# Rotary embedding of q and k: the swapped halves by DMA between SBUF partitions instead of a permutation matmul

## What is computed

```
def rope(x):                      # x[..., 64]
    x1, x2 = x[..., :32], x[..., 32:]
    return concatenate([x1 * cos - x2 * sin, x2 * cos + x1 * sin], axis=-1)

qa = rope(rms(aq, a_q_norm)); ka = rope(rms(ak, a_k_norm))   # 4 heads x 2 each
qc = rope(cq);                kc = rope(ck) * 64 ** -0.5     # 4 heads each
w  = softmax(qa0 ka0) - lam * softmax(qa1 ka1); y_a = rms(w @ va)
```

## Time and profile before

| | |
|---|---|
| median of the runs | 3362.06 us |
| the profiled execution, its own time | 3362.12 us |
| its span | 3360.3 us |
| PE busy | 3253.8 us, 97%, 14858 instructions |
| PE weight load busy | 2604.9 us, 78% |
| DVE busy | 1762.4 us, 52% |
| ACT busy | 1281.6 us, 38% |
| POOL busy | 28.7 us, 1% |
| mean granted TensorE clock | 0.986 |
| share of PE in the chain that ended last | 83% |
| HBM weight stream (q1) | 283.15 MB, 29.5% of 16 DMA engines |

### The profile page before, as it was taken

One profiled execution on the slowest core, in us unless ns is written; L12 is line 12 of the kernel. 1 busy time (PEld: TensorE's weight loads), 2 busy tenths in 40 slices (PEclk: granted clock), 3 DMA queues, 4 the chain that ended last, 5 costly groups with the idle time before them and its releaser, 6 DMA issues.

```text
span 3360.3 us, 37192 instructions
## 1 busy us (share of the span) xinstructions
PE 3253.8 (97%) x14858; PEld 2604.9 (78%) x14858; DVE 1762.4 (52%) x2893; ACT 1281.6 (38%) x1952; POOL 28.7 (1%) x57
## 2 busy tenths in 40 slices
PE   7999999999999999999999999999999986999998
PEld 6888877677788888888877677878888764878886
DVE  6333688645463336433487755364334665873333
ACT  4222446533342224322356544243233365343222
POOL 0000000000000000000000000000000000000000
PEclk9999999999999999999999999999999997999999
DMA  4333321222233332333222232323333542223332
GB/s 134 100 99 90 100 82 58 78 82 86 90 94 101 94 94 88 107 95 100 88 89 68 67 90 80 94 83 106 100 95 89 99 63 42 67 85 103 94 97 72
DMA packets 282077, 297.75 MB, mean 89 GB/s; under 512 B 9776, under 2 KB 270256, under 8 KB 281904
## 3 DMA queue, kind: packets, MB, share of 16 engines
q1 hardware_dynamic: 277408, 283.15, 29.5%
q0 software_dynamic: 3536, 10.55, 1.0%
q10 hardware_dynamic: 960, 1.67, 0.1%
HBM read 293.24 MB, written 2.10 MB: 88 GB/s over the span
## 4 chain that ended last, share of the span: by engine, by line
PE 83%; DVE 10%; ACT 5%; issue 1%; DMA 1%; DVEq 0%; SPq 0%; ACTq 0%
PE bank L218 83%; DVE k_sc L180 2%; ACT k_sc L214 2%; DVE k_wl L170 1%; DVE k_sc L170 1%; PE bank L224 1%; ACT k_wh L214 1%; ACT L208 1%; DVE k_sc L184 1%; DMA k_raw<-in_ffn_w_gate 0%; DVE k_sc L196 0%; DVE k_sm L175 0%; DVE k_x L180 0%; ACT k_sc L213 0%; DVE k_sc L175 0%
## 5 line engine op out<-in xcount | busy, mean ns | idle before, releaser
L170 DVE TENSOR_TENSOR k_wl<-k_raw,k_wh 128x1024 fp32r<-128x1024 f32 x545 | 654.5, 1204 | 1142.8 <-ACT k_wh L214 1140.1
L218 PE MATMUL bank<-k_xh,k_wh 128*128 128x512 f32 x2376 | 956.9, 403 | 3.8 <-ACT k_xh L214 1.6
L214 ACT ACTIVATE k_wh<-k_raw 128x1024 fp32r<-128x1024 f32 x545 | 563.6, 1039 | 973.3 <-PE bank L218 704.6
L218 PE MATMUL bank<-k_xl,k_wh 128*128 128x512 f32 x2376 | 927.6, 390 | 1.7 <-DVE k_xl L170 1.7
L218 PE MATMUL bank<-k_xh,k_wl 128*128 128x512 f32 x2376 | 927.6, 390 | 1.2 <-DVE k_wl L170 1.2
L218 PEld LDWEIGHTS bank<-k_xh,k_wh 128*128 128x128 f32 x2376 | 447.5, 188 | 116.1 <-issue 18.8
L218 PEld LDWEIGHTS bank<-k_xl,k_wh 128*128 128x128 f32 x2376 | 447.5, 188 | 98.3 <-issue 8.7
L218 PEld LDWEIGHTS bank<-k_xh,k_wl 128*128 128x128 f32 x2376 | 447.0, 188 | 96.6 <-DVE k_wl L170 1.6
L218 PE MATMUL bank<-k_uh,k_wh 128*128 128x512 f32 x512 | 206.0, 402 | 19.0 <-ACT k_uh L214 19.0
L218 PE MATMUL bank<-k_Gb,k_wh 128*128 128x512 f32 x704 | 218.2, 391 | 0.0
L218 PE MATMUL bank<-k_Ga,k_wh 128*128 128x512 f32 x704 | 218.2, 391 | 0.0
(11 more groups left out here) (312 smaller groups left out, 3687.6 us busy)
## 6 DMA issues: line engine op xcount, KB each, us to landing
k_raw<-in_w_in SPq DMA_DIRECT2D x153, 512.0 KB, 3.7
k_raw<-in_ffn_w_gate SPq DMA_DIRECT2D x88, 512.0 KB, 3.8
k_raw<-in_ffn_w_up SPq DMA_DIRECT2D x88, 512.0 KB, 3.8
k_raw<-in_ffn_w_down SPq DMA_DIRECT2D x80, 512.0 KB, 3.4
k_raw<-in_w_out SPq DMA_DIRECT2D x28, 512.0 KB, 3.4
k_raw<-in_w_gate SPq DMA_DIRECT2D x22, 512.0 KB, 3.8
k_raw<-in_w_up SPq DMA_DIRECT2D x22, 512.0 KB, 3.8
k_raw<-in_w_down SPq DMA_DIRECT2D x20, 512.0 KB, 3.4
```

Source lines behind the costliest of these rows:

```text
L170: return q.op(lambda e: e.tensor_tensor(out, a, b, op), cost(out))
L214: return self.A.op(lambda e: e.activation(out, a, f, bias=bias, scale=scale), c)
L218: fn = lambda e: e.matmul(out, l, r, start=start, stop=stop, skip_group_check=True)
```

## The change

The permutation matrix is gone from the constants. `rotate` now takes a scratch slot of SBUF (`SC`, ten slots) and one of three new swap slots, and issues four DMAs from GpSimd's queue, each copying 32 partitions by 512 elements (64 KB) from the tile into the scratch slot, with the 32-partition blocks exchanged in pairs. The planner books the landing 5.0 us after the end of the operation that wrote the tile, and the generator waits for it by `ready`. The sign moves into the sin table. The three DVE operations stay; the first now reads both operands from SBUF and none from PSUM. The scratch slot is held from the issue of the DMAs on; the PSUM bank isn't taken.

```
     def rotate(self, dst, t):
-        b, fb = yield from self.bank([t])
-        t0 = self.mm(fb + [t, self.t_const], b, self.perm, dst, True, True, inc=True)
-        yield
+        s, fs = yield from self.wait_slot(self.SC)
+        i, fi = yield from self.wait_slot(self.SWAP)
+        self.nswap[i] += 1
+        self.G.wait([t] + fs + fi)
+        sem = self.swapsem[i]
+        for r in range(0, P, 32):
+            a, b = s[r:r + 32, :], dst[r ^ 32:(r ^ 32) + 32, :]
+            self.G.run(lambda e, a=a, b=b: e.dma_start(a, b).then_inc(sem, 16))
+        t0 = (f"swap{i}", sem, 64 * self.nswap[i])
+        self.ends[(t0[0], t0[2])] = self.ends[(t[0], t[2])] + 5.0
+        yield from self.ready([t0])
         yield from self.calm()
-        s, fs = yield from self.wait_slot(self.SC)
-        t1 = self.tt([t0] + fs, s, b, self.sin, ALU.mult)
-        self.MB.put(b, [t1])
+        t1 = self.tt([t0, self.t_const], s, s, self.sin, ALU.mult)
+        self.SWAP.put(i, [t1])
         t2 = self.tt([t0, t], dst, dst, self.cos, ALU.mult)
...
+        self.swapsem = [self.mksem(f"s_swap{i}") for i in range(3)]
+        self.SWAP, self.nswap = Slots(range(3)), [0, 0, 0]
...
+    sin[(np.arange(P) % 64) < 32] *= -1.0
```

More of the change, by code:

```diff
@@ L48 @@
 VEC, NVEC = vec_layout()
-NCONST = 5 * 128 + 2 * 512
+NCONST = 4 * 128 + 2 * 512
 EVERYWHERE = (ACT.Copy, ACT.Square, ACT.Abs, ACT.Identity)
@@ L1528, in build @@
         self.WL = [tl(WLt, i, 1024) for i in range(SPLIT)]
-        self.ident, self.ones, self.bones, self.perm, self.tri = (C[:, i * P:(i + 1) * P] for i in range(5))
-        self.cos, self.sin = C[:, 640:1152], C[:, 1152:1664]
+        self.ident, self.ones, self.bones, self.tri = (C[:, i * P:(i + 1) * P] for i in range(4))
+        self.cos, self.sin = C[:, 512:1024], C[:, 1024:1536]
         self.vec, self.sm, self.sm2, self.sm3 = Vv[:, :], sm[:, :], sm2[:, :], sm3[:, :]
@@ L1628, in constants @@
     bones = np.kron(np.eye(2), np.ones((64, 64))).astype(f)
[L1629 to L1633, removed]
     tri = np.triu(np.ones((P, P))).astype(f)
@@ L1638, in constants @@
     sin = np.tile(np.sin(ang).T, (4, 1)).astype(f)
-    cpack = np.concatenate([ident, ones, bones, rot, tri, cos, sin], axis=1)
+    sin[(np.arange(P) % 64) < 32] *= -1.0
+    cpack = np.concatenate([ident, ones, bones, tri, cos, sin], axis=1)
     p, u = np.arange(P)[:, None], np.arange(T)[None, :]
```

## The result

The changed kernel takes **3382.98 us** (median of 4 runs, 3382.43 to 3386.43), the kernel before 3361.94 us beside it: ratio 1.0063, 95% interval 1.005 to 1.0076. The profiled execution spans 3380.9 us against 3360.3, so 20.6 of the 21.0 us between the medians show in it.

What follows compares the result with a forecast made beforehand. TensorE's work bounds the stretch, DVE's chain the flush. Layer 0: 41.4 - 15.6 - 16.7 = +9.1; layer 1: 39.8 - 13.4 - 16.7 = +9.7; +18.8 on 3362.1 gives 3381 us, range 3358 to 3396.

Steps and rivals of the forecast that it cites:

- The flush: From last w_in weight matmul to next stage: 15.6 grows to 41.4 us in layer 0, 13.4 to 39.8 in layer 1.
- Nobody waits for a swap: Stretch and flush: a swap takes 4.6 us, hidden behind DVE's other operations; DVE waits under 2 us in all.
- The stretch: Where w_in weight matmuls run: shorter by 8.7 us of rotations and 8.0 of moved work, 16.7 us per layer.
- Whatever is taken out of it comes back in full: In the stretch TensorE's work is the time: ten rotations of 0.87 us save 8.7 us per layer.
- the moved work: Score steps, transposes, a product with v and a sum go from stretch to flush: 8.0 us per layer.
- The cause of the move: q/k tiles come later by the swap and its planned 5 us; scores begin 54 weight matmuls later, 12.4 us.
- C: Experiments' theory: the planner no longer counts 0.85 us of TensorE work per rotation, so its calm test holds background steps back.
- Rival (a): Whole kernel: TensorE's work alone counts, swaps hidden, 20.9 us saved, 3341 us; chance 0.10.
- D: Experiments' theory: where PE waits for DVE, as at the stretch's start, TensorE work taken out brings nothing.
- Rival (b): Flush: DVE starts with 2 us on its list, not 6.8; each flush 8 us shorter, 3365 us; chance 0.14.
- Rival (c): Stretch and flush: swaps land late, at up to 9.9 us; +4 to +8 per layer, 3389 to 3397; chance 0.14.
- Foretold as signs: Layer 0: stretch ends near 572, flush 40 us, DVE busy over 80% of it, clock near 0.5; landings 2 to 3 us.

Runs made afterwards that it cites:

- kernel 2: The kernel before, with each rotation's matmul kept on the chip but not counted in the planner's TensorE clock (set back 0.85 us): 3396.8 us.
- kernel 1: The kernel before, matmuls kept, but each rotation goes on only 5.0 us of planned time after the norm that feeds it: 3358.7 us.
- kernel 7: The changed kernel with CALMX, the planner's lead bound while making the normed input's halves, raised from 3.5 to 4.0: 3349.7 us.
- kernel 4: The changed kernel without its 96 DMAs, halves not exchanged, the planner booking the same times: 3386.2 us.
- kernel 5: The kernel before with only branch C's four rotations per layer by DMA, attention A's eight kept as matmuls: 3365.2 us.
- kernels 6: The kernel before with only attention A's eight q and k rotations per layer by DMA, branch C's four kept as matmuls: 3393.8 us.
- 9: The changed kernel with CALMX 4.0 in place of 3.5, and CALM 4.0 in place of 3.0 from the third mixer on: 3336.6 us.
- kernels 3: The changed kernel with 0.85 us per swap added to the planner's TensorE clock, as if the matmul still stood there: 3364.9 us.
- 12: The changed kernel with 0.85 us per swap added to the planner's TensorE clock and two of four DVE operations cut from q/k norms: 3342.0 us.

## Why the prediction was right, and where it wasn't

The time was 3381 forecast, 3383 measured, and the likeliest case came about. The steps:

- **The flush**, the large term, held nearly point by point in layer 0. From its start DVE takes the first maximum at 6.2 us (6.8 worked out), is through with those of 384 at 20.0 (20.6), goes on with the norm at 24.1 (23.8) after standing 3.94 us (3.2), ends the last scaled addition at 33.6 (33.3), and the next stage starts at 41.4 (41.4). Two errors cancel at the end: the chain from the last transposes on took 7.76 us, not 7.2, and the 0.9 us for a weight load ahead of them isn't there, as they start when the addition ends, at 33.6. In layer 1 39.8 was worked out and 41.4 found: the end chain took 7.75 us, not 5.6, since the clock that had come back there before did not.
- **Nobody waits for a swap**: right. DVE is at the flush's two rotations at 11.3 and 15.4 us (11.9 and 16.0). The 4.6 us per swap were 3.3 and 3.9 for these two. In the stretch they were 5.1 to 6.4 for most of the swaps of branch A and one of C in each layer, above the 4.6 and the planned 5.0, with no effect either, since DVE had other operations first.
- **The stretch**, -16.7 per layer, was -16.1 and -17.8, but by two terms that were both off. "Whatever is taken out of it comes back in full" is wrong: of 8.7 us, DVE takes back 2.4 in either layer and in layer 0 the clock 1.7 more. And the moved work is more than 8.0: kernel 2, whose matmuls all stay, has a stretch 12.3 us shorter. 0.9 of that is one more sum in its flush, 1.7 are PE's waits of before that vanish (0.9, 0.6, 0.2); some 1.7 I can't place, but for a product with v that takes 2.47 us at full clock (layer 1 before, 1887.49) and not 2.05. The sum was right because the errors cancel, which is luck.
- **The cause of the move was wrong.** "A tile of q or k is ready later by the swap and its planned 5 us" explains nothing: kernel 1 books it as late, and its first scores come 12 weight matmuls earlier, not 54 later. That 54 weight matmuls lay between was read off the order, and that reading was sound; the reason was added by argument. It is C that the runs bear out.
- **Rival (a)**, 3341, failed as argued: the flush was over 32 us. What it describes is nearly kernel 7 less D. **Rival (b)**, a shorter list at the start of the flush: the list was 6.2 us long. **Rival (c)**, late swaps: half of the swaps were whole later than the forecast's 4.6 us, but none near the 9.9 of (c), none waited for, and no price shows in kernel 4. Its argument misread: these issues ran beside DVE operations of a few columns only, so they couldn't show an issue "whatever DVE does". The rule of the Trainium skill ("SBUF — State Buffer", "Who interferes with whom"), that DVE's two-port operations lock out the descriptors of a DMA from GpSimd, is hardly put to the test here: only 8 of the 96 issues overlap a copy or scaling of DVE with 128 columns or more, and these landed after 1.8 to 2.4 us. None of the 29 late ones does.
- Foretold as signs: last weight matmul near 572 (573.38), flush of 40 us (41.4), clock near 0.5 in most of it (0.73 at its head, 0.50 to 0.63 from 580 to 595 and from 600 on, 1.00 between). DVE busy in over 80% of the flush was wrong: it was 26.5 of 41.4 us, 64%, since it had nothing left in the last 7.8 and stood for ACT before. Of the landings, foretold at 2 to 3 us, 67 took 1.8 to 2.4 and 29 took 3.6 to 5.0. "It is wrong if the stretch has PE waits that weren't there": one such wait was there, and it was indeed the sign of a wrong term.

## What to carry to other kernels

When an ahead-of-time planner paces background work by an engine's planned time, taking work off that engine changes the order of everything else; read the new order first, and hide or add the count alone to see its price apart from the work's. Removed work is worth its length only while the engine stays the last to be ready: look a few microseconds behind each removal for who is waited for next. After such a change set the pacing anew before judging it, and that of the kernel before as well: here the same swap was 0.6% slower or, with one number altered, 0.4% faster, while the kernel without it gained 0.5% by one number too.

## What the runs showed of the hardware

A DMA from SBUF to SBUF of 32 partitions by 512 elements (64 KB) issued from POOL lands after 1.8 to 2.4 us, nearly as fast as the 16 KB ones of the earlier trace rows, unless a chunk of weights (512 KB) has just been issued. All 28 swap issues of the changed kernel that start 0.05 to 1.54 us after SyncE's issue of a chunk land after 3.6 to 5.0 us, within 1.2 us of the chunk's own landing; the chunk beside the swap at 443.48 is issued at 444.40, and of its four issues, at 443.48, 443.98, 444.47 and 444.96, the last two take over 4 us. Of the other 68 one does, issued 0.4 us ahead of a chunk. The profiled executions of kernels 6, 7 and 9 show the same (20, 5 and 5 issues within 1.6 us behind a chunk's, all at 3.7 us or more, and no other over 2.5); those of kernels 3 and 12 are less sharp, with 2.4 to 4.4 us behind a chunk's issue. So in these traces a small DMA's landing goes with what another engine's queue issued just before it. No run moves the chunks to show it as the cause.

And the same wait of PE may or may not cost its clock. In the profiled execution of the kernel before, two waits of 0.8 us near 902 are followed by half clock (windows as above):

```profile
902.00:904.00 2.00, 1.17 (x5) 0.84 (x5) 2.00 (x4) 2.00 (x5) 0.00 (x0) 0.92 0.00 0
904.00:906.00 2.00, 2.00 (x7) 1.54 (x6) 2.00 (x5) 2.00 (x4) 0.00 (x0) 0.50 0.00 0
906.00:908.00 2.00, 2.00 (x8) 1.63 (x7) 2.00 (x3) 0.12 (x1) 0.00 (x0) 0.72 0.00 0
```

In kernel 5, with the same two waits:

```profile
902.00:904.00 2.00, 1.70 (x7) 1.42 (x8) 2.00 (x5) 2.00 (x5) 0.00 (x0) 1.00 0.00 0
904.00:906.00 2.00, 2.00 (x10) 1.67 (x9) 2.00 (x5) 1.46 (x2) 0.00 (x0) 1.00 0.00 0
906.00:908.00 2.00, 2.00 (x10) 1.65 (x10) 1.59 (x2) 0.09 (x1) 0.00 (x0) 1.00 0.00 0
```

The one is 1.66 us longer there than the other. The 2.35 us wait of the changed kernel shows the same: behind it the clock falls in layer 0, and in layer 1, behind 2.34 us, it stays at 1.00, which is the 1.7 us by which the two stretches differ. So steps of about 1.7 us between two profiled executions say nothing of the kernels; I did not find what decides it.
